# A one-core hybrid layer with 32 experts: a new order of loads in the first stage, two-row runs of expert weights, routing in two parts, and a last stage inside the expert stage

## What is computed

```python
h = rms_norm(x, norm1_g) * (1 + scale1) + shift1
proj = h @ w_in                                   # 1024 x 2500
y = concat(rwkv7_time_mix(proj[:, :1792], ...),   # 8 heads of 64, a recurrence over the tokens
           dsa_mix(q, ckv, q_idx, k_idx, w_idx))  # attention over 256 chosen latent rows
x = x + (1 + gate1) * (y @ w_out)
h = rms_norm(x, norm2_g) * (1 + scale2) + shift2
g = argmax(h @ w_group + b_group)                 # 1 of 4 groups
e1, e2 = top2((h @ w_expert + b_expert)[group g]) # 2 of its 8 experts
moe = w1 * expert(e1, h) + w2 * expert(e2, h)     # expert: (silu(h @ gate) * (h @ up)) @ down
x = x + (1 + gate2) * moe
out = rms_norm(x, final_norm_g) * (1 + scale_f) + shift_f
```

## Time and profile before

| | us |
|---|---|
| runs, median (lowest to highest) | 1965.93 (1961.29 to 1966.78) |
| profiled execution, its own time | 1973.04 |
| its span, first to last instruction | 1971.1 |
| TensorE busy, share of the span | 1606.1, 81% |
| DVE, ACT, POOL busy | 871.0, 605.5, 399.5 |
| DMA over the span | 362.07 MB, mean 184 GB/s |

### The profile page before, as it was taken

The page is one execution under the profiler, slowest core; times in us unless marked ns, Lnnn a source line. Parts: engine busy times, 40 slices in busy tenths (PEclk is TensorE's granted clock), DMA queues, the critical chain, the costliest instruction groups (busy, mean ns, idle before and its releaser), DMA issues. The chain is left out here.

```text
span 1971.1 us, 40655 instructions
## 1 busy us (share of the span) xinstructions
PE 1606.1 (81%) x16134; PEld 1059.6 (54%) x16135; DVE 871.0 (44%) x1904; ACT 605.5 (31%) x1169; POOL 399.5 (20%) x825
## 2 busy tenths in 40 slices
PE   3899999867778888889876994677979997999920
PEld 2744444336667667667662453455656664666610
DVE  2158676356777866866641224111112221222228
ACT  3213887713334344444330221010111111111112
POOL 7330457701110110110100000110111111111133
PEclk8999999987999999999997995798989998999965
DMA  9493534320031001100005645499999999999655
GB/s 308 167 389 122 201 121 158 115 80 26 13 99 28 25 24 26 31 18 7 7 12 165 218 144 192 169 361 368 376 354 340 340 350 345 359 333 343 224 204 184
DMA packets 195983, 362.07 MB, mean 184 GB/s; under 512 B 29984, under 2 KB 67920, under 8 KB 195856
## 3 DMA queue, kind: packets, MB, share of 16 engines
q1 hardware_dynamic: 158128, 305.98, 44.9%
q0 software_dynamic: 37728, 54.34, 8.9%
HBM read 303.48 MB, written 56.64 MB: 183 GB/s over the span
## 5 line engine op out<-in xcount | busy, mean ns | idle before, releaser
L1868 PE MATMUL psX<-arena 128*64 128x256 f32 x1536 | 191.2, 406 | 49.8 <-DMA arena<-in_e_down_dram 47.9
L1868 PEld LDWEIGHTS psX<-arena 128*64 128x64 f32 x1536 | 120.9, 147 | 133.6 <-issue 90.2
L1892 PE MATMUL psP<-arena 128*64 128x512 f32 x768 | 175.4, 598 | 0.0
L1830 DVE SCALAR_TENSOR_TENSOR arena<-arena,psX 128x256 f32<-128x256 f32 x48 | 20.2, 421 | 346.1 <-ACT arena L1801 346.1
L792 PE MATMUL psX<-arena 128*128 128x512 f32 x320 | 142.6, 601 | 3.4 <-DVE arena L693 1.9
L1805 ACT ACTIVATE arena<-psP 128x512 f32<-128x512 f32 x48 | 28.7, 597 | 378.9 <-PE psP L1892 378.9
L487 ACT ACTIVATE arena<-arena 128x1024 bf16<-128x1024 f32 (+5 forms) x138 | 134.2, 973 | 32.5 <-POOL arena L444 28.6
L792 PE MATMUL psP<-arena 128*128 128x512 f32 x320 | 141.2, 595 | 2.9 <-DVE arena L693 2.9
L1779 POOL DMA_DIRECT2D expert_rows<-arena x48 | 41.7, 869 | 495.8 <-ACT arena L1805 466.9
L1673 PE MATMUL psP<-arena 128*128 128x512 f32 x256 | 116.0, 613 | 16.0 <-DMA arena<-mix_T 10.9
L1233 PE MATMUL psP<-ckvT,arena 128*128 128x512 f32 (+3 forms) x192 | 82.5, 542 | 33.9 <-DVE st L1072 22.6
(11 more groups left out here) (399 smaller groups left out, 2743.0 us busy)
## 6 DMA issues: line engine op xcount, KB each, us to landing
arena<-in_e_gate_dram SPq DMA_DIRECT2D x32, 2048.0 KB, 21.1
arena<-in_e_up_dram SPq DMA_DIRECT2D x32, 2048.0 KB, 26.6
arena<-in_e_down_dram SPq DMA_DIRECT2D x32, 2048.0 KB, 23.6
arena<-in_ada_w_dram SPq DMA_DIRECT2D x12, 2048.0 KB, 13.9
expert_rows<-Z POOLq DMA_DIRECT2D x34, 512.0 KB, 17.5
expert_rows<-arena POOLq DMA_DIRECT2D x48, 256.0 KB, 12.6
proj_T<-arena SPq DMA_DIRECT2D x36, 256.0 KB, 2.0
arena<-in_x_dram SPq DMA_DIRECT2D x16, 512.0 KB, 6.7
```

Of the source, the lines that this page charges most:

```text
L1830: dve.scalar_tensor_tensor(out=hid, in0=hid, scalar=1.0, in1=psum["X0"][:, 0:DE // 2], op0=ALU.add, op1=ALU.mult).then_inc(q("half_gated"), 1)
L1868: mm = pe.matmul(psum["X0"][BLK * h:BLK * h + BLK, 0:DE // 2], xT[:, k, :], gate_w[u][:, k, DE // 2 * h:DE // 2 * (h + 1)], start=(k == 0) ...
L1892: mm = pe.matmul(psum["P0"][BLK * half:BLK * half + BLK, :], hidT[:, f, h, :], down_w[u][:, KE // 2 * h + f, D // 2 * half:D // 2 * (half ...
```

## The change

Five parts, and some moves that they need.

1. **First stage.** An ada vector is cut by rows: each slot has 512 rows, four whole rows to a partition in runs of 1024 elements, and `ada` waits for the second slot only at its second half. The narrow columns of `w_in` group 0 become a load of their own, placed so that the 196 columns lie side by side: one matmul chain of 196 columns in place of 128 and 68. Both loads of group 0 wait until vector 1 has landed, group 1 waits for group 0. POOL builds its constants first and issues its small loads once vector 1 has landed.
2. **Mix and route.** In the mix stage SP writes two modulation rows to DRAM and reads them back paired (`pair_cols`), and loads tile 0 of `mix_T` into the place where route wants it. In route ACT takes the squares of the next tile early; the eight transposed pieces are split, four to DVE, four to ACT; the logits alternate between two banks; the last tile's transposes come ahead of `route(6)`; group and experts are picked for tiles 0 to 5 first, then for 6 and 7; the closing wait for expert weights goes, and two semaphores that outlive the stage are waited for in the expert stage.
3. **Expert weights.** Gate and up are loaded as pairs of rows, runs of 1024 elements; the transposes of the gathered rows read every second column to match.
4. **Expert rows.** The gate `1 + gate2` is multiplied when the result leaves PSUM, on DVE, where ACT copied it. The last block's store is issued by SP.
5. **Last stage.** No barrier before it: it stands at the end of the expert stage's programs. POOL issues all 16 gathers in a row with the powers between the later ones; TensorE weighs and sums the two rows with two diagonal matrices (made by ACT) into four banks in turn; DVE has one addition and two writing operations a tile.

```diff
-NROW = LATENT + CHUNK + IDX_HEADS
+NARROW = CHUNK + IDX_HEADS
+NROW = NARROW + LATENT
...
+            def four_rows(slot):
+                return slot.rearrange("p k n -> p (k n)").rearrange("p (a n) -> p a n", n=D)
...
-                        sp.dma_start(slots[s], ada_source(v)[0][:, 512 * h:512 * h + 512].rearrange("(k p) n -> p k n", p=P))\
+                        sp.dma_start(four_rows(slots[s]), ada_source(v)[0][512 * h:512 * h + 512, :].rearrange("(k p) n -> p k n", p=P))\
...
+                    if g == 0:
+                        sp.wait_ge(*at("slot_loaded3", "ada", 1))
+                        last = col + width - NARROW
+                        sp.dma_start(slots[0][:, :, 0:NARROW], w_in[0, :, last:last + NARROW].rearrange("(k p) n -> p k n", p=P)).then_inc(*sig("narrow_loaded", 0, by=16))
+                        sp.dma_start(slots[0][:, :, NARROW:width], w_in[0, :, col:last].rearrange("(k p) n -> p k n", p=P)).then_inc(*sig("slot_loaded0", "win", g, by=16))
+                        return
+                    if g == 1:
+                        sp.wait_ge(*at("slot_loaded0", "win", 0))
...
+                pool.wait_ge(*at("slot_loaded3", "ada", 1))
...
-                    for h in range(2):
-                        pe.wait_ge(*at(f"slot_loaded{ada_slot(v, h)}", "ada", v))
-                    per_slot = 512 // PART_COLS
                     for k in range(KD):
+                        h, row = divmod(k, KD // 2)
+                        if row == 0:
+                            pe.wait_ge(*at(f"slot_loaded{ada_slot(v, h)}", "ada", v))
                         for q_ in range(PARTS):
+                            mm = pe.matmul(psum[f"W{v % 2}"][rows_of(q_), 0:PART_COLS], cB[:, k, :], four_rows(slots[ada_slot(v, h)])[:, row, cols_of(q_)],
                                            start=(k == 0), stop=(k == KD - 1))
                     mm.then_inc(*sig("ada_done", v))
 
...
-                        pe.matmul(psum[b][:, 0:LATENT], hT[:, k, P * t:P * t + P], w[:, k, 0:LATENT],
-                                  start=(k == 0), stop=(k == KD - 1))
-                    for k in range(KD):
-                        mm = pe.matmul(psum[b][:, LATENT:NROW], hT[:, k, P * t:P * t + P], w[:, k, LATENT + 256:452],
-                                       start=(k == 0), stop=(k == KD - 1))
...
+                    if t == NT - 1:
+                        sp.wait_ge(*at("nat_b", NT - 1))
+                        sp.wait_ge(*at("v_turned", NT - 1))
+                        sp.wait_ge(*at("dsa_stored", 0))
+                        sp.wait_ge(*at("rwkv_stored", 0))
+                        sp.dma_start(next_mix, mix_d[:, :, tile(0)].rearrange("c p s -> p c s")).then_inc(*sig("next_mix", 0, by=16))
...
-                    sp.dma_start(dst, src[0, e].rearrange("(k p) n -> p k n", p=P)).then_inc(*sig("weights_loaded", *(("next", e, src is e_up, src is e_down)), by=16))
+                    rows_of = src[0, e].rearrange("(k p) n -> p k n", p=P) if src is e_down else src[0, e].rearrange("(k p r) n -> p k r n", p=P, r=2)
+                    sp.dma_start(dst if src is e_down else by_pairs(dst), rows_of).then_inc(held[e == 1 and src is e_down], 16)
...
-                sp.wait_ge(*at("weights_loaded", "next", 1, False, True))
...
+                squares(0)
+                for t in range(NT):
+                    if t + 1 < NT:
+                        squares(t + 1)
+                    if t >= 2:
+                        act.wait_ge(*at("logits", t - 2))
+                    act.wait_ge(*at("xn_turned", t, 1))
+                    for k in range(KD // 2, KD):
+                        link(act, act.activation(kt(h2T, t)[:, k, :], g4(psum["T1"])[:, k % 4, :], ACT.Identity,
+                                                 bias=mod_cols[:, 2, k:k + 1], scale=mod_cols[:, 3, k:k + 1]), "h2T_high", t, k)
+                for a, b in PARTS_OF:
...
+                def low_half(t):
+                    if t >= 2:
+                        dve.wait_ge(*at("logits", t - 2))
+                    dve.wait_ge(*at("xn_turned", t, 0))
+                    for k in range(KD // 2):
+                        link(dve, dve.tensor_scalar(kt(h2T, t)[:, k, :], g4(psum["T0"])[:, k, :], mod_cols[:, 3, k:k + 1], mod_cols[:, 2, k:k + 1], ALU.mult, ALU.add),
+                             "h2T_low", t, k)
...
+                low_half(NT - 2)
+                chosen = choose(*PARTS_OF[0])
+                next(chosen)
+                low_half(NT - 1)
+                next(chosen)
+                weights(*PARTS_OF[0])
...
                         project_out(t + 1)
+                    if t == NT - 1:
+                        turn(t)
                     if t:
                         route(t - 1)
...
-                    sp.dma_start(gate_w[u], e_gate[0, bass.ds(e, 1)].rearrange("a (k p) n -> p (a k) n", p=P)).then_inc(q(f"gate_loaded{u}"), 16)
+                    sp.dma_start(by_pairs(gate_w[u]), e_gate[0, bass.ds(e, 1)].rearrange("a (k p r) n -> p (a k) r n", p=P, r=2)).then_inc(q(f"gate_loaded{u}"), 16)
...
+                pairs = sp.value_load(first_block[0:1, NE + 1:NE + 2], min_val=NE // 2, max_val=MAX_BLOCKS // 2)
+                full = sp.value_load(first_block[0:1, NE + 2:NE + 3], min_val=NE // 2 - 1, max_val=MAX_BLOCKS // 2)
+                sp.wait_ge(q("y_ready"), pairs * 2 + 1)
+                sp.dma_start(y_d[bass.ds((full * 2 + 1) * BLK, BLK), :].rearrange("r (h n) -> h r n", h=2), y_sb[1]).then_inc(q("last_stored"), 16)
+                def load_x1(t):
+                    sp.dma_start(x1[:, t, :], x1_d[tile(t), :]).then_inc(*sig(f"x1_loaded{t}", 0, by=16))
+                sp.wait_ge(q("last_stored"), 16)
+                for t in range(3):
+                    load_x1(t)
+                for t in range(NT):
+                    if t + 3 < NT:
+                        load_x1(t + 3)
+                    sp.wait_ge(*at("out", t))
+                    sp.dma_start(out[0, tile(t), :], first[:, t, :]).then_inc(*sig("out_stored", t, by=16))
+                sp.wait_ge(*at("out_stored", NT - 1))
...
+                gather(pairs * 2 + 1, 1, pairs * 2)
+                store(full * 2, 0)
+                gather(pairs * 2 + 2, 0, pairs * 2 + 1)
                 pool.wait_ge(q("gathered0"), (pairs + 2) * 16)
                 pool.wait_ge(q("gathered1"), (pairs + 1) * 16)
 
+                pool.wait_ge(q("y_stored0"), pairs * 16)
+                pool.wait_ge(q("y_stored1"), full * 16)
+                pool.wait_ge(q("last_stored"), 16)
+                pool.sem_inc(q("stores_seen"))
+                for t in range(NT):
+                    for j, dst in enumerate((first, second)):
+                        pool.indirect_dma_start(dst[:, t, :], None, y_d[:, :], bass.IndirectOffsetOnAxis(ap=dest[:, t, j:j + 1], axis=0))\
+                            .then_inc(*sig(f"gathered{j}{t}", 0, by=16))
+                    if t >= 4:
+                        roots(t - 4)
+                for t in range(NT - 4, NT):
+                    roots(t)
...
+                for t in range(NT):
+                    for j in range(2):
+                        link(act, act.activation(weigh[:, t, j, :], ident[:, :], ACT.Copy, scale=wgt[:, t, j:j + 1]), "weights", t, j)
...
+                def evict(b, j, stored):
+                    dve.wait_ge(q("y_done"), b + 2)
+                    if stored is not None:
+                        dve.wait_ge(q(f"y_stored{j}"), stored)
+                    dve.tensor_tensor(y_sb[j], psum["P0"], gate_half, ALU.mult).then_inc(q("y_ready"), 1)
...
+                def add(t):
+                    dve.wait_ge(*at("combined", t))
+                    dve.wait_ge(*at(f"x1_loaded{t}", 0))
+                    if t >= 2:
+                        dve.wait_ge(*at("x_squares", t - 2))
+                    link(dve, dve.tensor_tensor(res[:, t % 2, :], psum["PTXW"[t % 4]], x1[:, t, :], ALU.add), "x2", t)
...
+                def write(t):
+                    b = t % 2
+                    dve.wait_ge(*at("x_rstd", t))
+                    if t == 0:
+                        dve.wait_ge(*at("rows_loaded", 3))
+                    step(dve.scalar_tensor_tensor(out=first[:, t, :], in0=res[:, b, :], scalar=s_x[:, 16 + t:17 + t], in1=gain_row, op0=ALU.mult, op1=ALU.mult))
+                    link(dve, dve.tensor_tensor(first[:, t, :], first[:, t, :], shift_row, ALU.add), "out", t)
+                add(0)
+                variance(0)
+                for t in range(NT):
+                    if t + 1 < NT:
+                        add(t + 1)
+                    write(t)
+                    if t + 1 < NT:
+                        variance(t + 1)
...
-                        mm = pe.transpose(psum["T0"][:, BLK * k:BLK * k + BLK], rows[:, P * k:P * k + P], ident[BLK:P, BLK:P])
+                        mm = pe.transpose(psum["T0"][:, BLK * k:BLK * k + BLK], rows.rearrange("r (k p i) -> r k i p", p=P, i=2)[:, k // 2, k % 2, :], ident[BLK:P, BLK:P])
```

(10 more changed lines are left out.)

379 lines of the change are left out of this document (179 added, 200 removed).

## The result

The changed kernel took a median of 1907.1 us (1906.2 to 1909.9, four runs) against 1966.4 (1961.3 to 1967.3) before: a ratio of 0.969, with a 95% interval of 0.966 to 0.972. It is faster by 59 us, not by the 89 forecast, and lies above the range of 1855 to 1902. Its profiled execution took 1907.3 us, span 1905.3.

What follows compares the result with a forecast made beforehand. TensorE was taken to bound the project stage, TensorE and DMA closely together the expert stage. Terms summed to 88.9 us off the profiled 1973.0, giving 1884.1; less 7.1 for the median, 1877 us, range 1855 to 1902.

Steps and rivals of the forecast that it cites:

- First stage, start: Start of the project stage: vector 1 lands near 34.5 and the w_in rows begin at 47, gaining 14.3 us.
- Row products: First stage: one chain of 196 columns takes 2.69 us a tile instead of 3.58; eight tiles save 7.1 us.
- Route, head and tail with the closing wait: Route: earlier first product 5 us, earlier counts and table 11.2, no wait for expert weights at its end 7.7.
- The closing wait: End of route: dropping the wait for expert weights, which took 7.7 us, gains 7.7.
- Mix stage: Between 427 and 1043 us: work unchanged, its few new transfers counted at nothing.
- Expert stage: Longer gate and up runs save 0.78 us an expert and one stall, 17 us; strided transposes counted at nothing.
- Last store: End of the expert stage: SP's 256 KB store lands in 3.3 us, so the first gather follows sooner, gaining 8.4 us.
- Last stage: From first gather to end: 55.2 us instead of 73.4, with 4.5 us a tile on DVE, gaining 18.2.
- the first: Expert stage: longer runs bring the loads nothing as the engines' total decides; 17 us goes, 1894 us; chance 15%.
- The second: Last stage: TensorE stays at 1.2 GHz, 7.0 us a tile, 17.5 us more, 1894 us; chance 10%.
- The third: Expert stage: all waits for weights vanish and the clock is kept, 11 us more gained, 1866 us; chance 10%.
- The fourth: Expert stage: 4 KB load packets lengthen POOL's gather landings, costing beyond 20.7 us; slower than before, 2003 us at 28; chance 4%.

Runs made afterwards that it cites:

- joined_a: copy_sorts with group 0 of w_in no longer waiting for vector 1, and the shift and gain rows loaded behind the last expert's weights; 1893.4 us.
- one_row_held: one_row with the wait for down of expert 1 back at the end of route, and the shift and gain rows loaded behind the last expert; 1932.2 us.
- one_row: The change with gate and up loaded in single rows (2 KB runs) and the transposes reading contiguous columns; 1927.1 us.
- one_row_sbuf: one_row with 448 bytes of padding ahead of the arena in SBUF; 1910.2 us.
- copy_sorts: The change with ACT's copy sorting the gathered rows' columns, so that the transposes read contiguously; 4 KB runs kept; 1900.9 us.
- joined_e: joined_a with each expert-row store issued as two of 64 rows, the paired-rows DRAM tensor declared last and 288 bytes of padding; 1859.3 us.
- joined_d: joined_a with each expert-row store issued as two of 64 rows, the paired-rows DRAM tensor declared last and 448 bytes of padding; 1864.0 us.

## Why the prediction was wrong

The forecast was 30 us too low: the sum of 88.9 came out as 65.8 on the profiled executions, 23 less, and the 7.1 us that I took off because the profiled execution before lay above its median was not there after (1907.3 against 1907.1). The second profile of the kernel before was 1974.1 again, but single runs of that kernel beside the experiments reached 1980.3, so both lie within its own spread and nothing is to be taken off for profiling.

- **First stage, start** (14.3; was 9.0, below its end of 10). Vector 1 landed 3.8 us later than 12.6 MB at 418 GB/s gave. Between 10 and 36 us the rate was near 400, but the first 10 us moved only 223 GB/s, and from 36 to 38 us a tail came at 62 GB/s and a DMA share of 0.21. The landing of `w_in`, from a row, held (13.5 against 13.1). The wait that the change adds cost 5.9 us of it (joined_a); I had priced it in and not asked what it was worth.
- **Row products** (7.1; was 6.8): right, by the step forecast.
- **Route, head and tail with the closing wait** (23.9; was 23.0): head and tail right, by the steps forecast. The closing wait (7.7) was worth some 4.1 (one_row_held against one_row, one execution each): the first gather comes 6.3 us earlier without it, but the step from it to the gate matmul takes 2.2 longer, the +2.0 of the table.
- **Mix stage** (0; was 3.6): the spread between executions, no merit of the change.
- **Expert stage** (17; was 2.9). The step that failed is "the stride in the transposes' input I count at nothing". It added 22.2 us to TensorE, 8.4 to the time. A second cause is one that I did not see: the 64-byte shift of the arena, 3.5 us here (not clear of noise) and 16 with one-row loads. The term itself was near in size: longer runs gain 15 us when the arena lies where it lay, and 26 at the shifted place. 15 less 8.4 less 3.5 is 3.1, from one_row_sbuf to the change. That 2.9 was measured is closer than the traces allow: against the second profile of the kernel before, with its stage of 634.3, it is 8.1.
- **Last store** (8.4; was 3.2). I priced it by stores of equal size and another shape. Its own kind had a row, 12.6 us at the median, and the very store of 1886.21 had taken 9.1 from issue to landing.
- **Last stage** (18.2; was 19.1): right, with small errors that cancel in part. The first output came 20.6 us after the first gather (20 forecast), a tile took 4.0 (4.5), but the sixth tile's addition waited 2.1 us for x.

Of the rivals, the first (longer runs bring nothing) is refuted by copy_sorts against one_row, which bears out the windows of the earlier trace rows (388 against 418 GB/s) and not the rule that the prediction took from the Trainium skill (DMA: Bandwidth & Descriptors, Specifications), by which both would load alike. The second is refuted by the rows of 3.60 us: they are the price at 2.4 GHz; only the first tile, after 17.6 us of idle time, was slower, 5.38 us. The third did not come, 26.6 us of waits stayed. The fourth has its mechanism right in direction. Over the whole span the gathers' median landing rose from 12.7 to 15.2 us; it was 12.7 in one_row, with 2 KB runs, and 15.2 in copy_sorts, with 4 KB runs. It stayed under the 20.7 from which it would have cost. (The 12.6 that the prediction used is the stores' landing, not the gathers'.) Beneath all of them lay what none named: the bound that I read as "loads at a share of 0.96" was in part the way the stage's stores were issued, each at the share of two engines (0.12 to 0.13 where one was alone), with POOL's small packets besides.

## What to carry to other kernels

- When a layout of data is changed to please the loads, cost its reader on the busiest engine, instruction by instruction; a copy on an idle engine can take the sorting over.
- Price a transfer by rows of its own shape. A share near one eighth while only one transfer is on the way says that it keeps two of the 16 engines busy; look at the slowest dimension of its pattern before taking a stage for bound by bandwidth.
- Where two resources share a bound, each repair alone shows a part of its worth. Repeat the pair before calling one of them harmless.

## What the runs showed of the hardware

- Weight loads of 64 x 128 float32 that read every second column took 215 ns where contiguous ones took 139.
- Moving the destination of all loads by 64 bytes within a partition (from byte 61600 to 61664) cost 16 to 17 us with 2 KB runs (345 against 353 GB/s) and 3.5 (not clear of noise) to 5.7 us with 4 KB runs. Once the stores were split, 1.4 us was left, within the ranges. Why is not shown; starts at a multiple of 512 bytes (joined_e) and at the old place (joined_d) could not be told apart.
- A store over two halves of 64 partitions moved at 40 GB/s with a DMA share of 0.12 to 0.13; as two stores of 64 rows it landed in 2.3 us instead of 7.7, and the gathers that ran beside such stores landed in 6.9 instead of 15.3.
- A store of the same shape issued by POOL had 528 packets, 464 of them under 512 B; the split ones were 432 packets fewer for each store.
- Gathers of 64 rows by POOL landed in 12.7 us at the median beside weight loads with 2 KB runs (one_row) and in 15.2 beside 4 KB runs (copy_sorts).
